# Modulation panels in plain fp32 over four column groups, one long chunk on TensorE instead of two, four slots of split weights

## The reference, cut to what matters

```python
def modulation(cond, w, b):                      # w: 1024 x 6144, for each of two layers
    m = jax.nn.silu(cond) @ w + b
    return m.reshape(cond.shape[:-1] + (N_MOD, D_MODEL))

    m_l = modulation(c, mod_w[l], mod_b[l])[:, :, None, :]     # two conditions, c and c_ctx,
    m_c = modulation(c_ctx, mod_w[l], mod_b[l])                # share the same weights
    hl = rmsnorm(xl, norm_mix_g[l]) * (1.0 + m_l[:, 1]) + m_l[:, 0]
    ...
    pl = hl @ w_in                               # even_mixer: 256 + 256 tokens, 1024 -> 5152
    xbc = jax.nn.silu(dwconv(p_state[..., :SSD_CONV_DIM], conv_w, conv_b))     # 5 taps, 2048 channels
    u = v * jax.nn.sigmoid(gate)
    u = dwconv(u, dw_w, dw_b)                    # 31 taps, 1024 channels, rows of 64 tokens
```

## Time and profile before

| | before |
|---|---|
| median of 3 runs | 3507.75 us (3507.65 to 3509.22) |
| profiled execution, its own time | 3507.16 us |
| its span, first to last instruction | 3505.4 us |
| TensorE busy | 2989.0 us, 85% |
| VectorE busy | 2094.8 us, 60% |
| ScalarE busy | 1623.2 us, 46% |
| mean granted TensorE clock | 0.919 of full speed |

### The profile page before, as it was taken

How to read it: one execution, slowest core, us unless ns; L and a number is a source line. 1 busy time by engine, 2 the same in 40 slices (tenths; PEclk the granted TensorE clock), 3 DMA queues, 4 the chain that set the end, 5 groups by cost and what they waited for, 6 DMA issues and landing times. The chain is left out here.

```text
span 3505.4 us, 37572 instructions
## 1 busy us (share of the span) xinstructions
PE 2989.0 (85%) x13600; PEld 2304.8 (66%) x13600; DVE 2094.8 (60%) x3131; ACT 1623.2 (46%) x2478; POOL 267.5 (8%) x224
## 2 busy tenths in 40 slices
PE   5999977685999977988579997988589999777798
PEld 2666646473888866438468885876368787666686
DVE  4797756644899963116679995532555554146554
ACT  5444444322888852012358885431254443115543
POOL 1000003300111100005001100001000000020000
PEclk8999988897999988999789998999689999969999
DMA  5444430022999242210179955532034454300252
GB/s 221 156 156 144 144 132 1 1 92 85 363 412 410 87 150 85 93 75 1 52 281 411 412 212 190 192 137 104 2 143 182 155 196 165 146 28 1 108 189 94
DMA packets 96375, 544.06 MB, mean 155 GB/s; under 512 B 11073, under 2 KB 12481, under 8 KB 72641
## 3 DMA queue, kind: packets, MB, share of 16 engines
q1 hardware_dynamic: 88128, 512.05, 38.4%
q0 software_dynamic: 7776, 28.32, 2.2%
q10 hardware_dynamic: 288, 1.31, 0.1%
HBM read 578.33 MB, written 26.21 MB: 172 GB/s over the span
## 5 line engine op out<-in xcount | busy, mean ns | idle before, releaser
L1192 PE MATMUL ps<-w_hi,x_hi 128*128 128x512 f32 x1440 | 577.0, 401 | 16.6 <-DVE w_lo L2159 8.1
L1193 PE MATMUL ps<-w_lo,x_hi 128*128 128x512 f32 x1440 | 567.4, 394 | 0.0
L1194 PE MATMUL ps<-w_hi,x_lo 128*128 128x512 f32 x1440 | 567.0, 394 | 0.0
L1192 PEld LDWEIGHTS ps<-w_hi,x_hi 128*128 128x128 f32 x1440 | 274.6, 191 | 74.0 <-DVE w_lo L2159 8.5
L1194 PEld LDWEIGHTS ps<-w_hi,x_lo 128*128 128x128 f32 x1440 | 274.4, 191 | 59.6
L1193 PEld LDWEIGHTS ps<-w_lo,x_hi 128*128 128x128 f32 x1440 | 275.1, 191 | 55.1
L1192 PE MATMUL ps<-x_hi,w_hi 128*128 128x512 f32 (+1 forms) x512 | 219.3, 428 | 73.5 <-DVE w_lo L804 38.4
L1192 PE MATMUL ps<-w_hi,hidden_hi 128*128 128x512 f32 x688 | 271.5, 395 | 9.5 <-DVE hidden_lo L2326 6.0
L1194 PE MATMUL ps<-w_hi,hidden_lo 128*128 128x512 f32 x688 | 268.2, 390 | 0.0
L1193 PE MATMUL ps<-w_lo,hidden_hi 128*128 128x512 f32 x688 | 267.9, 389 | 0.0
L1537 DVE TENSOR_TENSOR w_lo<-weights_A,w_hi 128x1024 fp32r<-128x1024 f32 x168 | 204.4, 1220 | 37.0 <-ACT w_hi L1468 34.4
(11 more groups left out here) (512 smaller groups left out, 5611.8 us busy)
## 6 DMA issues: line engine op xcount, KB each, us to landing
weights_A<-in_moe_gate SPq DMA_DIRECT2D x160, 512.0 KB
weights_B<-in_moe_up SPq DMA_DIRECT2D x160, 512.0 KB
weights_A<-in_ffn_gu SPq DMA_DIRECT2D x24, 2048.0 KB, 7.5
weights_C<-in_moe_down SPq DMA_DIRECT2D x80, 512.0 KB
weights_D<-in_moe_down SPq DMA_DIRECT2D x80, 512.0 KB
weights_B<-in_ffn_gu SPq DMA_DIRECT2D x20, 2048.0 KB, 7.5
weights_C<-in_ffn_down SPq DMA_DIRECT2D x24, 1024.0 KB, 6.4
y_slots<-tile_out SPq DMA_DIRECT2D x42, 512.0 KB, 7.6
```

The lines of the kernel that those rows point to most:

```text
L1192: nc.tensor.matmul(out, w_hi, x_hi, start=first, stop=False)
L1193: nc.tensor.matmul(out, w_hi, x_lo, start=False, stop=False)
L1194: return nc.tensor.matmul(out, w_lo, x_hi, start=False, stop=last)
```

## The change

In both stages the modulation weights are no longer split. TensorE reads them from the ring's areas as plain fp32, with the two conditions `cond` as stationary operand. Of the eight blocks of 128 rows of a panel, block k writes to partitions 32 * (k % 4) and the next, that is to the k % 4th of four column groups of the array, and the second four add to the first four. So the bank has to be cleared once, the row copies take 128 partitions, and `pair_sum` has 128 rows and adds the four groups up.

In `even_in` one `modulate` now stands behind each first piece of a chunk, for half a panel; SP's loads of C and D wait for it. The split of weight pieces is made three pieces ahead in four slots. Chunk 6 of the long convolution moves from TensorE to VectorE, as a single chunk of which two taps count as one step, late in `WORK`.

```diff
-            with stage(nc, "vec_in cst_in x_in eps_set zeroed silu_done cond_hi cond_lo hi_done lo_done used rows_copied turned added scaled") as (block, s):
+            rows = self.sb(ctx, "modulation_rows", [P, 2, 512])
+            with stage(nc, "vec_in cst_in x_in eps_set cleared silu_done used rows_copied turned added scaled") as (block, s):
...
-                    ring.load(sp, "A", 4, s["lo_done"])
-                    ring.load(sp, "B", 8, s["lo_done"])
+                    ring.load(sp, "A", 1, s["used"])
+                    ring.load(sp, "B", 2, s["used"])
                     ring.load(sp, "C", None)
                     ring.load(sp, "D", None)
                     sp.dma_start(self.X[:].rearrange("p k t -> p (k t)"), d["x"]).then_inc(s["x_in"], 16)
-                    ring.load(sp, "A", 12, s["lo_done"])
-                    ring.load(sp, "B", 16, s["lo_done"])
+                    ring.load(sp, "A", 3, s["used"])
+                    ring.load(sp, "B", 4, s["used"])
...
+                    for q in range(4):
+                        area = "AB"[q % 2]
+                        ring.arrived(pe, area)
+                        if q >= 2:
                             pe.wait_ge(s["rows_copied"], q - 1)
-                        for c in range(2):
-                            k, cols = 2 * j + c, slice(c * 512, (c + 1) * 512)
-                            nc.tensor.matmul(ps[0:4, q % 2, :], CC[:, k, :], wh[:, n % 4, cols], start=(k == 0), stop=False)
-                            last = nc.tensor.matmul(ps[0:4, q % 2, :], CZ[:, k, :], wl[:, n % 4, cols], start=False, stop=(k == KD - 1))
+                        for k in range(KD):
+                            j = k % 4
+                            last = nc.tensor.matmul(ps[32 * j:32 * j + 2, q % 2, :], cond[:, k, :],
+                                                    ring.buf[area][:, k * 512:(k + 1) * 512], start=(k < 4), stop=(k >= 4))
                         last.then_inc(s["used"], 1)
-                        if j == 2 and q:
+                        if q:
                             turn(q - 1)
...
-        ON_PE, ON_DVE = (6, 7), (0, 2, 4)
+        ON_PE, ON_DVE = (7,), (0, 1, 2, 3, 4, 5, 6)
...
-            SLOTS, AHEAD = 2, 1
-            FIRST, MS, MPIECES, NPIECE = 4, 3, 160, 80
+            SLOTS, AHEAD = 4, 3
+            FIRST, NPIECE = 4, 80
...
-                total = len(ON_DVE) * K31 + 8 * K5
+                total = len(ON_DVE) * K31 // 2 + 8 * K5
                 return max(0, min(total, (p - 9) * total // (NPIECE - 10)))
 
-            WORK = [("long", 0), ("long", 2), ("state", 0), ("state", 2), ("long", 4), ("state", 4), ("state", 6), ("state", 8),
-                    ("state", 10), ("state", 12), ("state", 14)]
+            WORK = [("long", (0, 1)), ("long", (2, 3)), ("state", (0, 1)), ("state", (2, 3)), ("long", (4, 5)), ("state", (4, 5)),
+                    ("state", (6, 7)), ("state", (8, 9)), ("state", (10, 11)), ("long", (6,)), ("state", (12, 13)), ("state", (14, 15))]
...
-                    def modulate(m):
-                        q, k = divmod(m, KD)
-                        pe.wait_ge(s["m_lo"], m + 1)
-                        if k == 0 and q >= 2:
+                    def modulate(h):
+
+                        q, half = divmod(h, 2)
+                        pe.wait_ge(ring.landed["CD"[half]], 16 * (used["CD"[half]] + q + 1))
+                        if h == 0:
+                            pe.wait_ge(s["m_cleared"], 1)
+                        if half == 0 and q >= 2:
                             pe.wait_ge(s["m_rows"], q - 1)
-                        nc.tensor.matmul(ps[0:4, MB + q % 2, :], CC[:, k, :], mhi(m), start=(k == 0), stop=False)
-                        nc.tensor.matmul(ps[0:4, MB + q % 2, :], CZ[:, k, :], mlo(m), start=False, stop=(k == KD - 1)).then_inc(s["m_used"], 1)
+                        for j in range(4):
+                            last = nc.tensor.matmul(ps[32 * j:32 * j + 2, MB + q % 2, :], self.cond[:, 4 * half + j, :],
+                                                    ring.buf["CD"[half]][:, j * 512:(j + 1) * 512], start=(half == 0), stop=(half == 1))
+                        last.then_inc(s["m_used"], 1)
...
-                                                    self.c("pair_sum", 2, 4), start=True, stop=True)
+                                                    self.c("pair_sum", 2), start=True, stop=True)
...
-                        modulate(2 * p)
-                        modulate(2 * p + 1)
+                        if half == 0:
+                            modulate(n)
...
-                            ring.load(sp, "CD"[h % 2], 4 * (4 * i + h) + 4, s["m_lo"])
+                            ring.load(sp, "CD"[h % 2], 4 * i + h + 1, s["m_used"])
                         ring.load(sp, area, 8 * (i + 1), s["lo_done"])
...
-                        nc.scalar.activation(mrows, ps[0:4, MB + q % 2, :], ACT.Copy).then_inc(s["m_rows"], 1)
+                        nc.scalar.activation(mrows, ps[:, MB + q % 2, :], ACT.Copy).then_inc(s["m_rows"], 1)
...
-                        if p + 1 < NPIECE:
-                            hi(p + 1)
-                        for m in (2 * p + 2, 2 * p + 3):
-                            if m < MPIECES:
-                                m_hi(m)
+                        if p + AHEAD < NPIECE:
+                            hi(p + AHEAD)
...
+                        if len(chunks) == 2 or j % 2:
+                            yield
...
-                        if p + 1 < NPIECE:
-                            lo(p + 1)
-                        for m in (2 * p + 2, 2 * p + 3):
-                            if m < MPIECES:
-                                m_lo(m)
+                        if p + AHEAD < NPIECE:
+                            lo(p + AHEAD)
...
-    put("pair_sum", np.tile(np.eye(2), (2, 1)))
+    put("pair_sum", np.tile(np.eye(32)[:, 0:2], (4, 1)))
```

More of the change, by code:

```diff
@@ L231, in _ @@
                                          ACT.Silu).then_inc(s["silu_done"], 1)
[L232 to L238, removed]
+                    for q in range(4):
+                        act.wait_ge(s["used"], q + 1)
@@ L239, in copy_rows @@
                         if q >= 2:
                             act.wait_ge(s["turned"], q - 1)
[L241 to L251, removed]
@@ L259, in _ @@
[L259 to L265, removed]
@@ L266, in _ @@
-                    for q in (2, 3):
+                    dve.wait_ge(s["vec_in"], 16)
+                    for q in range(4):
                         self.add_bias(dve, q, ps[:, 2 + q % 2, 0:8], s["turned"], q + 1, s["added"])
@@ L561, in dve_taps @@
             def dve_taps(p):
-                total = len(ON_DVE) * K31 + 8 * K5
+                total = len(ON_DVE) * K31 // 2 + 8 * K5
                 return max(0, min(total, (p - 9) * total // (NPIECE - 10)))
-            WORK = [("long", 0), ("long", 2), ("state", 0), ("state", 2), ("long", 4), ("state", 4), ("state", 6), ("state", 8),
-                    ("state", 10), ("state", 12), ("state", 14)]
-            STARTS, STATE_TAPS, STATE_STEPS, at, step = [], {}, {}, 0, 0
-            for kind, c in WORK:
+            WORK = [("long", (0, 1)), ("long", (2, 3)), ("state", (0, 1)), ("state", (2, 3)), ("long", (4, 5)), ("state", (4, 5)),
+                    ("state", (6, 7)), ("state", (8, 9)), ("state", (10, 11)), ("long", (6,)), ("state", (12, 13)), ("state", (14, 15))]
+            STARTS, STATE_TAPS, at, step = [], {}, 0, 0
+            for kind, chunks in WORK:
                 STARTS.append(at)
-                at += 2 * (K31 if kind == "long" else K5)
-                step += K31 if kind == "long" else K5
+                at += len(chunks) * (K31 if kind == "long" else K5)
+                step += K31 * len(chunks) // 2 if kind == "long" else K5
                 if kind == "state":
-                    STATE_TAPS[c // 2], STATE_STEPS[c // 2] = at, step
+                    STATE_TAPS[chunks[0] // 2] = at, step
             for a in "AB":
@@ L700, in state_silu @@
                     def state_silu(c):
-                        act.wait_ge(s["tap"], STATE_TAPS[c // 2] - 1 + c % 2)
+                        act.wait_ge(s["tap"], STATE_TAPS[c // 2][0] - 1 + c % 2)
                         nc.scalar.activation(XBC[:, c, :, 2:2 + SEQ], acc[:, c % 2, :].rearrange("p (s t) -> p s t", s=2),
                                              ACT.Silu).then_inc(s["xbc_out"], 1)
-                    hi(0)
-                    m_hi(0)
-                    m_hi(1)
+                    for p in range(AHEAD):
+                        hi(p)
                     taken = silus = 0
@@ L743, in _ @@
                             taken += 1
-                        while silus < 16 and dve_taps(p) >= STATE_STEPS[silus // 2]:
+                        while silus < 16 and dve_taps(p) >= STATE_TAPS[silus // 2][1]:
                             state_silu(silus)
@@ L793, in all_taps @@
                 def all_taps(dve):
```

(4 more changed lines are left out.)

82 lines of the change are left out of this document (24 added, 58 removed).

## The result

| | before | after |
|---|---|---|
| median of 4 runs | 3507.7 us | 3421.3 us (3418.5 to 3423.1) |
| ratio | | 0.9755, 95% interval 0.9743 to 0.9766 |
| profiled execution, its own time | 3507.16 us | 3423.12 us |
| its span | 3505.4 us | 3421.3 us |
| TensorE, VectorE, ScalarE busy | 2989, 2095, 1623 us | 2921, 2002, 1514 us |

The kernel is 86.4 us faster, 2.5%; 3425 was forecast. The two profiled executions differ by 84.0 us, and all but 2 us of that lies ahead of 411 us. The last 2.1 us are in work that is the same in both and are no more than runs of one kernel differ by.

What follows compares the result with a forecast made beforehand. TensorE was taken as the bound, VectorE from 140 to 220 us. Products 218.0, modulation 46.6, dt 8.8, turns 18.6, taps 26.8 and residue 9 made 327.8 against 409.6; with 0.4 in the first stage, 82.2 saved: 3425 us, range 3412 to 3463.

Steps and rivals of the forecast that it cites:

- Bound and balance: even_in: TensorE busiest, VectorE setting the pace from 140 to 220 us; after the change VectorE never slower on the mean.
- The modulation: even_in: 320 split products, 74.4 us, become 40 groups of four fp32 matmuls at 1.17, 46.6 us.
- 1.39 a group: Modulation in even_in: alternative estimate from the skill's page, 3.46/3.17 + 0.30, making the sum 9 us longer, near 3434.
- Taps: even_in: 31 of 62 diagonal matmuls leave TensorE for VectorE; 26.8 us stay and 26.8 go.
- Lead: even_in: weight splits three pieces ahead in four slots cover VectorE's silu waits of 3.65 us; a few us of waits remain.
- The residue: even_in: of 36.2 us, 9 are left for lower clock, small gaps at turns and taps, and a few us of waits.
- the 36.2 that were called waits: even_in before the change: the part of 409.6 us beyond the 373.4 of terms; waits, lower clock and small gaps.
- First stage: Stage before even_in: activations' load issued within 1 us of where it was; gain 0.4 us.
- sign of a misread stage: Start of even_in: a first product later than 73.5 would mean that the first stage was misread.
- The third: Modulation groups don't overlap at all: 3.76 a group, 3535 us, slower than before; chance 0.08.
- the first: Modulation: only two column groups run at once, 2.03 a group, first stage 2.5 longer, 3460 us; chance 0.14.
- The second: even_in: VectorE becomes the bound, lead used up by piece 31, five silu waits come through, 18 us: 3443; chance 0.13.

Runs made afterwards that it cites:

- idle splits: Changed kernel with the 160 ScalarE copies and 160 VectorE subtractions of modulation pieces put back in even_in as work nobody reads: 3472.7 us, 0.9890 of before.
- the last run: Changed kernel with activations' load first, constants awaited only before the first turn, and all long taps on VectorE: 3400.5 us, 0.9691 of before.
- the first experiment: Changed kernel with all blocks of a modulation panel written to one column group, in both stages: 3532.6 us, 1.0075 of before.

## Why the prediction was right, point by point

**Bound and balance.** That VectorE, "not TensorE, sets the pace" from 140 to 220 us before the change is what the earlier trace rows show. The idle splits show that the relief of VectorE and ScalarE matters: with their old load of splits and everything else changed, even_in is 42 us longer and the kernel 47 to 51 slower, more than half of the 86 us. Two limits go with it. VectorE has the 31 taps of chunk 6 in that run, 20.5 us that it didn't have before the change, so the run doesn't give what the relief alone was worth in the old kernel; idle splits with chunk 6 left on TensorE were not run. And it puts back both engines' work at once, so their shares aren't told apart.

**The modulation.** Forecast 74.4 to 46.6 us, at 1.17 a group; measured 1.17 and 40 x 1.17 = 46.8. The two ends that no row had showed were 3.72 and 2.00 where the working had 3.76 and 2.03. So the fixed part of 0.30, taken over from matmuls of another shape, was right to 0.04. Why there is one is not shown. From the figure of the Trainium skill ("TensorE: Matmul & The Clock Gate", Part 3, 2.38 times for three column tiles) I had estimated 1.39 a group and a sum of 3434. The trace agrees with the efficiency, carried over to four, if it is taken to hold the fixed part: a group takes 3.72/1.17 = 3.2 times less than in one column group, where I had 3.17. My 1.39 counted the fixed part a second time. Without it the group takes four times less.

**Taps.** 26.8 us forecast; putting them back costs 31 x 0.87 = 27.0 in TensorE's timeline and 23.1 in the time. VectorE was level with TensorE from 140 to 220 us, as forecast, and had slack after it.

**Lead.** "A few us of waits" for TensorE: none for a weight split after the start.

**The residue.** This is the term that was furthest off: 9 us forecast, 2.6 found. From 80.40, the start of the first group, to 405.62 are 325.2 us; products 79 x 2.80 = 221.2, groups 46.8, dt 11.1, turns 19 x 0.88 = 16.7 and taps 26.8 make 322.6. Nearly all of the rest is the lower clock: from 99.53 to 105.08, behind the dt product, thirteen products take 5.55 us instead of 3.03. So the trace leaves hardly anything for waits and gaps of TensorE.

**Luck.** The sum was 327.8 against the 325.2 measured, and its terms miss in both directions: residue -6.4, turns -1.9, products +3.2 (0.233 instead of 0.230), dt +2.3, groups +0.2. The dt product, which I had called unchanged, is the same work at a lower granted clock, 0.63 against 0.80; in the other profiled kernels it took anything from 8.2 to 11.2, so that is no effect of the change. The first group started at 80.40 and not 79.05, 1.35 later, and the tail was 1.2 longer (5.3 against 4.15). So 81.9 us are gained up to the next stage, with 82.2 forecast, though the single terms are off by up to 6.4. The turn before the change was undercounted as well: by the same reading as above it was 1.18 us (124.51 to 127.08, less two products and the four modulation products), not 0.98, so 4 us more of the 36.2 that were called waits were turns.

**First stage.** Costed at a gain of 0.4; the norm started 0.66 earlier. That is right for a wrong reason: the load of the activations was issued 3.2 us earlier and not within 1 us, and the reload of A ahead of it 4.5 later; the two cancel. The sign of a misread stage, a first product of even_in later than 73.5, did appear, with 74.98. But it was set too low: the kernel before already had 73.94. The product came 1.0 later because the norm's matmuls took 10.45 us against 9.17, at a granted clock of 0.70 against 0.82, between TensorE's levels of 1.2 and 2.4 GHz. TensorE stood idle for 5.6 us ahead of them and before the change for 1.9, but the idle time doesn't explain it, as two more runs show (before, after, the last run, all long taps on VectorE):

```profile
44.75 9.17 PE L356 MATMUL ps<-squares,constants 128*128 128x512 f32 x16 [1.90 <-ACT squares L341]
...
44.09 10.45 PE L321 MATMUL ps<-squares,constants 128*128 128x512 f32 x16 [5.58 <-ACT squares L306]
...
34.86 10.35 PE L322 MATMUL ps<-squares,constants 128*128 128x512 f32 x16 [1.87 <-ACT squares L307]
...
44.44 9.71 PE L321 MATMUL ps<-squares,constants 128*128 128x512 f32 x16 [7.64 <-ACT squares L306]
```

So these 1.3 us are scatter of the clock, whose cause is open. Another 0.4 is the clearing of PSUM, 0.91 us on VectorE ahead of the first weight split, of which ScalarE's first copy covers half; I had called it covered.

**Rivals.** The third, no overlap, has its time in the first experiment, 3532.6 against 3535; the first, two at once, 3459.6 against 3460; neither is what happened. The second, VectorE's waits coming through, is nearly the run with one piece of lead, 3441.9 against 3443, though that run takes the lead away and the rival had it used up; with three the waits are there and nobody waits behind them.

## What to carry to other kernels

Count what an operation costs on every engine, not on the one that it is for: the split of a modulation piece cost 0.60 us on VectorE and its two products 0.47 on TensorE, and an operation that is slower by itself can win by needing no preparation. A product with few stationary columns takes as long as a full one (0.23 us with 4 columns as with 128); laid over several column groups, each with its own block of the contraction, that time is spent once for all of them. A lead in slots hides the waits of an engine that has slack to catch up; on an engine that is full it hides little. And read a price up to the second instruction behind a piece of work, where the first one still pays for it: the short reading makes these groups look a tenth cheaper than they are.

## What the runs showed of the hardware that was not expected

- Four plain fp32 matmuls of 512 columns in four column groups take 1.17 us, the same passes in one group 3.72, in two 2.00. All three hold a fixed part of 0.26 to 0.31 us, the one with a single column group too, so it isn't a price of using several. The old modulation products, fp32r with 4 stationary columns, had none: four took 0.93.
- The same fp32r products had a pitch of 0.230 us before and 0.233 after. With two slots, and with two chunks on TensorE, it is 0.233 too, so neither of these made it. No run tells what did.
- The same dt product took 8.2 to 11.2 us in the profiled executions, by the granted clock (0.87 to 0.62).
- The turn's matmuls with 128 partitions of rows take 0.88 us, those with 4 took 1.18.
